# RWKV-7 and latent-attention mixers of a two-block model: deeper slots, smaller tiles, another order of the engines' work

## The reference

```python
def step(state, inp):                      # RWKV-7, 16 heads of 64, over 256 tokens
    r_t, w_t, k_t, v_t, a_t, b_t = inp
    sa = jnp.einsum('bhvk,bhk->bhv', state, a_t)
    state = (state * w_t[:, :, None, :]
             + sa[..., None] * b_t[:, :, None, :]
             + v_t[..., None] * k_t[:, :, None, :])
    return state, jnp.einsum('bhvk,bhk->bhv', state, r_t)

y = rwkv7_scan(r, decay, k, v, -kk, kk * a)        # then group norm, bonus, gate g
sc = (einsum(q_nope, k_nope) + einsum(q_pe, k_pe)) * scale     # MLA, 8 heads of 128
p = jax.nn.softmax(jnp.where(causal, sc, NEG_INF), axis=-1)
outs.append(jnp.einsum('bhqk,bkhd->bqhd', p.astype(v.dtype), v[:, :q1]))
x = x + jnp.concatenate([y_rwkv, y_mla], axis=-1) @ w_out[l]
```

## Time and profile before

| what | value |
|---|---|
| median of 3 runs | 2172.3 us |
| the profiled execution's own time | 2172.27 us |
| its span, first to last instruction | 2170.5 us |
| PE busy | 2147.1 us, 99% |
| DVE, ACT, POOL busy | 1689.5, 1089.1, 547.7 us |
| granted clock of PE | 0.999 of full |
| mixers stage | about 1223 to 1303 us |
| chain stage | about 1303 to 1325 us |

### The profile page before, as it was taken

How to read it: one execution, slowest core, us unless ns; L and a number is a source line. 1 busy time by engine, 2 the same in 40 slices (tenths; PEclk the granted TensorE clock), 3 DMA queues, 4 the chain that set the end, 5 groups by cost and what they waited for, 6 DMA issues and landing times.

```text
span 2170.5 us, 39431 instructions
## 1 busy us (share of the span) xinstructions
PE 2147.1 (99%) x14918; PEld 1881.1 (87%) x14918; DVE 1689.5 (78%) x2802; ACT 1089.1 (50%) x1489; POOL 547.7 (25%) x225
## 2 busy tenths in 40 slices
PE   8999999999999999999999999999999999999998
PEld 6888888888888888899999987888888888888887
DVE  7799778885899688788888656788888874547887
ACT  6555564445555564556554765443443443334454
POOL 4776731018677630210000623100000000000001
PEclk9999999999999999999999999999999999999999
DMA  7555445555545455554445302555555555555554
GB/s 260 189 177 182 163 175 177 191 192 196 189 170 184 152 184 184 185 205 159 159 165 188 118 25 97 193 178 190 191 180 190 192 181 189 193 181 187 193 213 175
DMA packets 69964, 384.82 MB, mean 177 GB/s; under 512 B 15376, under 2 KB 23056, under 8 KB 25168
## 3 DMA queue, kind: packets, MB, share of 16 engines
q1 hardware_dynamic: 69840, 383.09, 49.9%
HBM read 379.89 MB, written 3.18 MB: 176 GB/s over the span
## 4 chain that ended last, share of the span: by engine, by line
PE 71%; POOL 14%; issue 10%; DVE 2%; ACT 1%; DMA 1%; SPq 0%; POOLq 0%; DVEq 0%; ACTq 0%
PE ps L258 34%; PE ps L259 18%; POOL low L240 14%; PE ps L246 4%; PE ps L247 4%; PE ps L248 4%; PE ps L261 2%; DMA raw<-weights_dram 1%; PE ps L1898 0%; PE ps L1879 0%; PE ps L1865 0%; PE ps L1889 0%; PE ps L1939 0%; PE ps L2253 0%; PE ps L2255 0%
## 5 line engine op out<-in xcount | busy, mean ns | idle before, releaser
L258 PE MATMUL ps<-opA,whi 128*128 128x512 f32 x2460 | 871.2, 394 | 0.0
L259 PE MATMUL ps<-opA,low 128*128 128x256 f32 x2624 | 706.7, 279 | 0.2 <-DVE opA L1031 0.2
L228 ACT ACTIVATE whi<-raw 128x2048 fp32r<-128x2048 f32 x346 | 660.3, 1909 | 79.3 <-DMA raw<-weights_dram 78.0
L233 DVE TENSOR_TENSOR low<-raw,whi 128x2048 fp32r<-128x2048 f32 x252 | 583.4, 2315 | 65.0 <-ACT whi L228 51.2
L258 PEld LDWEIGHTS ps<-opA,whi 128*128 128x128 f32 x2460 | 461.1, 187 | 106.0 <-issue 3.0
L240 POOL TENSOR_TENSOR low<-raw,whi 128x2048 fp32r<-128x2048 f32 x94 | 432.0, 4613 | 408.0 <-ACT whi L228 378.7
L259 PEld LDWEIGHTS ps<-opA,low 128*128 128x128 f32 x2624 | 492.0, 187 | 14.6 <-DVE opA L1031 0.5
L258 PE MATMUL ps<-opB,whi 128*128 128x512 f32 x1380 | 493.3, 397 | 3.2 <-DVE small L1141 1.4
L259 PE MATMUL ps<-opB,low 128*128 128x256 f32 x1472 | 397.1, 280 | 0.0
L258 PEld LDWEIGHTS ps<-opB,whi 128*128 128x128 f32 x1380 | 259.4, 188 | 67.8 <-issue 5.0
L267 ACT ACTIVATE crossed<-ps 128x256 f32<-128x256 f32 x167 | 64.2, 384 | 488.7 <-PE ps L261 488.6
(11 more groups left out here) (431 smaller groups left out, 2583.1 us busy)
## 6 DMA issues: line engine op xcount, KB each, us to landing
raw<-weights_dram SPq DMA_DIRECT2D x348, 1024.0 KB, 4.8
bias_t<-table_dram SPq DMA_DIRECT2D x16, 384.0 KB, 5.9
raw<-weights_dram SPq DMA_DIRECT2D x4, 512.0 KB, 8.1
hT<-xT_dram SPq DMA_DIRECT2D x4, 512.0 KB, 8.3
lora_g<-lora_dram SPq DMA_DIRECT2D x1, 1024.0 KB, 5.0
out_dram<-y_tok SPq DMA_DIRECT2D x4, 256.0 KB, 2.4
out_dram<-hT SPq DMA_DIRECT2D x3, 256.0 KB, 2.7
p_in<-pT_dram SPq DMA_DIRECT2D x2, 256.0 KB, 5.8
```

The source lines that it names most:

```text
L228: act.activation(whi[:, v % RING, :], raw[:, v % RING, :], ACT.Copy).then_inc(hi_done.sem, 1)
L233: v_.tensor_tensor(wlo(v % RING, 0, width), raw[:, v % RING, 0:width], whi[:, v % RING, 0:width].bitcast(F32), ALU.subtract).then_inc(lo_d ...
L258: pe.matmul(*cross, start=start, stop=False)
L259: mm = pe.matmul(ps[:, b, 0:T], wlo(s, w0, w0 + P), op[:, k, 0:T], start=False, stop=False)
```

## The change

`keyed_values` of items 2 to 15 uses 32x32 tiles on the diagonal (the rest of the masked matrix is zero). `within_scores` takes its second and third operand, `kk` and `r_`, in one product of 64 columns; for that `kk` and `uS` become parts of one tile. The order inside the slots is another on PE, ACT and DVE: within-chunk scores are made two pairs ahead, `keyed_values` and `exps` one slot ahead, `turned` stands between the two keyed groups, `values` between the reads, and `steps(s)` ends slot s. The waits follow the new order. `gate_rows` is issued a slot later. An exponential of one element is put before the `k_pad` copy of the mix stage. The first state of the chain is copied once the first of the last four `step_out` is done, behind two `step_in`; the last `values` moves into the chain, behind the first next state, and the wait for the last store moves to the first `gates`.

```diff
@@ phase_mix, ACT
                 evict_block(6, 2)
+                act.activation(small[:, 3:4], small[:, 7:8], ACT.Exp)
                 act.wait_ge(*mx["k_rope"](1))
@@ phase_mixers, PE: within_scores, keyed_values, solved, reads, steps
-                        for x, (w, z) in enumerate(((a_gate, r_), (k_, kk), (k_, r_))):
+                        for x, w in enumerate((a_gate, k_)):
...
-                                    mm = pe.matmul(ps[CH * c:CH * c + CH, 3 + h, at:at + CH], w[head[h], pair, t], z[head[h], pair, t], start=True, stop=True)
+                                    z = kk_uS[head[h], pair:pair + apart + 1:apart, t] if x else r_[head[h], pair, t]
+                                    mm = pe.matmul(ps[CH * c:CH * c + CH, 3 + h, at:at + CH + CH * x], w[head[h], pair, t], z, start=True, stop=True)
...
-                        pe.wait_ge(*wi["ry_read"](n - 1))
+                        pe.wait_ge(*wi["aq_read"](n - 1))
...
+                        for c in range(4):
+                            t = slice(CH * c, CH * c + CH)
+                            mm = pe.matmul(ps[t, mine[y], cols], scm[t, pair % 2, y, h, 1, t], tokV[t, pair % 2, y, cols], start=True, stop=True)
...
+                    if n >= 2:
+                        pe.wait_ge(*wi["ry_read"](n - 1))
...
+                    if n + 2 < 2 * RW_B:
+                        pe.wait_ge(*wi["G_read"](n + 3))
...
+                    pe.wait_ge(*ml["probsT_read"](pair + 1))
                     if pair:
                         pe.wait_ge(*ml["stored"](pair))
...
+                    if pair + 1 < RW_B:
+                        pe.wait_ge(*ml["biased"](pair + 2))
@@ phase_mixers, ACT: order
+                keyed_read(0)
+                keyed_read(1)
+                exps(0)
+                scaled(0)
                 for s in range(RW_B):
                     more = s + 1 < RW_B
-                    keyed_read(2 * s)
-                    keyed_read(2 * s + 1)
-                    exps(s)
                     if s:
                         step_out(s - 1, 0)
                     solved_read(2 * s)
-                    solved_read(2 * s + 1)
                     if s:
                         step_out(s - 1, 1)
+                    solved_read(2 * s + 1)
                     if more:
                         tokens_read(2 * s + 2)
-                    scaled(s)
                     if s:
                         step_out(s - 1, 2)
                         step_out(s - 1, 3)
+                    if s in (3, 4):
+                        gate_rows(s - 3)
                     if more:
                         tokens_read(2 * s + 3)
+                        keyed_read(2 * s + 2)
+                        keyed_read(2 * s + 3)
+                        exps(s + 1)
...
-                    if s in (2, 3):
-                        gate_rows(s - 2)
+                    if more:
+                        scaled(s + 1)
@@ phase_mixers, DVE: order
                 biased(0)
+                masked(2)
+                masked(3)
+                finished(0)
...
-                    finished(s)
+                        if more:
+                            masked(2 * s + 3)
                     if more:
                         biased(s + 1)
-                        masked(2 * s + 2)
...
                     reads(2 * s)
+                    if s + 2 < RW_B:
+                        masked(2 * s + 4)
                     if more:
-                        masked(2 * s + 3)
+                        finished(s + 1)
                     reads(2 * s + 1)
...
-                for c in range(4):
-                    step_in(RW_B - 1, c)
+                step_in(RW_B - 1, 0)
+                step_in(RW_B - 1, 1)
+                v.wait_ge(*wi["held"](4 * (RW_B - 1) + 1))
+                v.wait_ge(*ml["outT"](MLA_H - 1))
+                v.tensor_copy(state[:, 1, :, :], step_n[:, 0, :, 0:DH]).then_inc(ch["state"].sem, 1)
+                step_in(RW_B - 1, 2)
+                step_in(RW_B - 1, 3)
@@ phase_chain, PE
+                        if c == 1 and todo == "next":
+                            last_values()
@@ phase_chain, DVE
                         v.wait_ge(*ch["next"](c))
+                        if c < 4:
+                            v.wait_ge(*wi["held"](4 * (RW_B - 1) + c + 1))
```

More of the change, by code:

```diff
@@ L1210, in program @@
         second = area + 2 * KB * T
-        uS = place("uS", [P, IN2_UNITS, T], at=arena)
+        apart = (arena - area) // T - 8
+        kk_uS = place("kk_uS", [P, apart + IN2_UNITS, T], at=area + 8 * T)
+        uS = kk_uS[:, apart:apart + IN2_UNITS, :]
         r_, k_, v_ = uS[:, 0:8, :], uS[:, 8:16, :], uS[:, 16:24, :]
@@ L1217, in program @@
         a_gate = place("a_gate", [P, RW_B, T], at=area)
-        kk = place("kk", [P, RW_B, T], at=area + 8 * T)
+        kk = kk_uS[:, 0:RW_B, :]
         bonus = place("bonus", [P, RW_B, T], at=area + 16 * T)
@@ L1790, in program @@
         step_n = uS[:, 8:24, :].rearrange("p (s n) t -> p s n t", s=2)
+        state = place("state", [P, 2, 2, RW_B, DH], at=second + 8 * T)[:, :, 0, :, :]
         def phase_mixers(u_next, op):
@@ L1976, in _ @@
                         scores(s + 1)
-                        within_scores(s + 1)
+                        tokens(2 * s + 3)
+                    if s + 2 < RW_B:
+                        within_scores(s + 2)
+                    if more:
+                        keyed_values(2 * s + 2)
+                    turned(s)
+                    if more:
+                        keyed_values(2 * s + 3)
                     reads(2 * s)
-                    if more:
-                        tokens(2 * s + 3)
-                    reads(2 * s + 1)
-                    turned(s)
                     if s:
                         values(s - 1)
-                steps(RW_B - 1)
+                    reads(2 * s + 1)
+                    steps(s)
                 pe.wait_ge(*ch["mla_lo"](1))
                 early_products(pe, u_next, 0, range(8, 12), op)
-                values(MLA_H - 1)
             @stage.scalar
@@ L2238, in gates, with last_values @@
                     mm.then_inc(ch["g"].sem, 1)
-                pe.wait_ge(*ml["stored"](MLA_H))
+                def last_values():
+                    pe.wait_ge(*ml["probsT_read"](MLA_H))
+                    pe.wait_ge(*ml["stored"](MLA_H - 1))
+                    pe.wait_ge(*wi["held"](4 * (RW_B - 1) + 3))
+                    pe.matmul(ps[:, 0, 0:T], vM[:, 0, 7 * P:8 * P], pTm[:, 1, 0:2, :], start=True, stop=False)
+                    mm = pe.matmul(ps[:, 0, P:T], vM[:, 1, 7 * P:8 * P], pTm[:, 1, 2, :], start=False, stop=True)
+                    mm.then_inc(ml["outT"].sem, 1)
                 for c in range(1, NCH):
@@ L2269, in _ @@
             def _(v):
-                v.wait_ge(*wi["held"](4 * RW_B))
-                v.wait_ge(*ml["outT"](MLA_H - 1))
-                v.tensor_copy(state[:, 1, :, :], step_n[:, 0, :, 0:DH]).then_inc(ch["state"].sem, 1)
                 v.wait_ge(*gs["w_hi"](2))
```

24 lines of the change are left out of this document (12 added, 12 removed).

## The result

The changed kernel takes 2178.2 us (median of 11 runs, 2175.6 to 2179.17), beside 2172.4 us for the kernel before on the same chip (11 runs, 2171.76 to 2173.94): a ratio of 1.0024, 95% interval 1.0016 to 1.0032. That is 5.8 us slower, where 0.8 faster was forecast, and outside the range. The profiled execution took 2178.3 us with a span of 2176.5.

A forecast was written before the change was run, and what follows sets the result against it. The prediction took TensorE (PE), busy for 99% of the span at full clock, to bound the kernel. Its terms, -4.4 + 0.2 + 2.7 - 1.2 + 1.9 = -0.8, gave 2171.5 us, range 2168.9 to 2174.3.

The forecast's parts named there:

- at nothing: Parts forecast to cost nothing: later gate rows, masked() further ahead, POOL's ends, one SP load, state's placement, kk joined to uS.
- 6, end of mixers: From solved(14) to the chain's first product: 7.9 us instead of 9.1, the last store's wait gone; -1.2 us.
- 1, keyed products: Keyed products of 14 items as 32x32 tiles: 0.22 us an item, 0.44 instead of 0.94 a slot, 0.50 saved.
- Rival A: Tiles don't run side by side: each keyed item costs 0.49 us, +3.8 over 14 items, 2175.3 us; 12%.
- 2, joined within-scores: Two within-score products joined, 32 products for 48: 0.72 us instead of 0.95 a slot, 0.23 saved.
- 3, order: Order in the slot: 0.21 us saved on step_out's wait, 0.20 lost to two more shape changes; period 9.05.
- 4, slot 6: Slot 6 has no within-scores left (-0.7), but steps(6) waits for store(5) behind ACT (+0.9); +0.2 us.
- 5, start: Start of the mixers: early exponential table load delays within-scores(0) by 1.1, tokens(3) waits about 0.9 for ACT; +2.7 us.
- 7, in the chain: Last values behind the chain's first product delay ACT's last store and first gate_w: 2.3 less 0.4 slack, +1.9 us.
- rival C: The chain's gate path has more slack than read, so its +1.9 falls away: -2.7, giving 2169.6 us; 10%.

The follow-up runs named there:

- lora_probs: The changed kernel with the gate's 1 MB load released by the turned probabilities of head 6, some 1.4 us later; 2174.16 us.
- pool_waits: lora_probs with POOL's subtraction into gw_stack held back until the chain's first state is copied; 2173.45 us.
- stack_early: lora_probs with ACT's gw_stack copy moved ahead of the store of the seventh head; 2174.19 us.
- gate_first: pool_waits with ACT doing the chain's first two gate_w pairs ahead of the two weight splits and the logarithm's table load; 2172.4 us.
- stack_gate: gate_first without the early exponential, and with ACT's gw_stack copy moved earlier in place of POOL's wait for the state; 2171.79 us.
- lora_outT: The changed kernel with the gate's 1 MB load released by the values of head 5, some 3.5 us later; 2174.24 us.
- before_gate_first: The kernel before, with ACT doing the first two gate_w pairs ahead of the two splits and the logarithm's table load; 2172.89 us beside 2172.62.
- values_first: lora_probs with the last values ahead of the chain's first next-state products instead of behind them; 2175.52 us.
- full_keyed: lora_probs with the keyed products of all 16 items full-size instead of in 32x32 tiles; 2179.27 us.
- gate_full: gate_first without the early exponential, all keyed products full-size, the gate's load behind the values of the sixth head; 2179.77 us.
- lora_halves: The changed kernel with the gate's 1 MB load in two of 0.5 MB, the second behind the values of the sixth head; 2175.1 us.
- before_lora_probs: The kernel before, with the gate's load released by the turned probabilities of head 6 instead of the scores of head 7; 2174.31 us.

## Why the prediction was wrong, step by step

**The loads, put at nothing, failed.** Under "at nothing" the prediction names one load, "SP's load behind the eighth mn, which leaves and lands about 1 us sooner"; that one did no harm. The load for the gate I did not look at: it too leaves at another point of PE's stream. I asked of the loads only when their data are wanted, and never what else uses the DMA engines. The price is 4.0 us, lora_probs against the change: 1.5 of PE's standstill, the rest the half clock behind it (from solved(14) to the state copy 10.11 us, 1295.87 to 1305.98, against 7.56 in lora_probs, 1294.34 to 1301.90). In the kernel before the packet came at 1288.3 and the load at 1289.8, so nothing in that trace spoke of it, but both were in it, 1.5 us apart.

With the load out of the way the time would have been 2174.2, inside the range, but not by the forecast's own sum: it lies 2.7 above it. The terms beside the load are compared in two stretches:

| stretch, us | before | forecast | change | lora_probs | pool_waits | stack_early | gate_first | stack_gate |
|---|---|---|---|---|---|---|---|---|
| solved(14) to the chain's first product | 9.12 | 7.9 | 11.96 | 9.41 | 8.05 | 9.03 | 8.04 | 9.04 |
| from there to the last kk | 20.31 | 22.2 | 22.47 | 22.45 | 22.45 | 22.45 | 21.95 | 21.30 |

**6, end of mixers (-1.2): the state copy mis-sized.** I took 0.5 us for the copy with its signal; it took 1.79. From the copy's start to the first product 1.85 us passed where I had 0.6. With the load out of the way the stretch is 0.3 longer than before (9.41) where I had it 1.2 shorter; with the copy at 0.43 it takes 8.05, close to the forecast's 7.9. I had moved a DVE operation by 1 us and not looked at what POOL does there. That the copy alone is not the price, but any DVE operation that meets POOL's, stack_early showed (9.03 with the copy at 0.43 and gw_lo at 2.21).

**1, keyed products (0.50 a slot): the size off.** An item costs 0.36 with the change of shape behind it, where I had 0.22 and 0.10, and the change ahead of turned 0.14 where I had 0.10. Of a gain of 0.30 (0.50 less two changes) 0.13 is left. Rival A was nearer, by another mechanism: the tiles cost less than its 0.49 an item, but the rest of the slot gives the gain back.

**2, joined within-scores (0.72):** right; 1242.02 to 1242.76 in lora_outT is 0.74. **3, order:** right in the best slots: a period of 9.09 (1276.11 to 1285.20 in the change) where I had 9.05. But the mean was 9.24, +0.95 over five periods. The first three took 9.34, 9.38 and 9.29; compared with slot 4 and 5, PE starts score products 0.2 to 0.3 us later in each of them, and one of these delays shows as a hole at issue (0.13 us at 1250.20). I had not expected such delays.

**4, slot 6 (+0.2):** steps(6) waited 0.44 us for ACT where I had 0.9, and its period is 8.96 in lora_probs where I had 9.25. **5, start (+2.7):** the waits came as forecast. Within-scores(0) wait 0.94 for the eviction, tokens(3) 1.14 for ACT:

```profile
1224.87 0.28 PE L1884 MATMUL ps<-kk_uS,a_gate 64*32 64x32 f32 x13 [0.94 <-ACT qT L1361]
...
1233.36 0.33 PE L1869 MATMUL ps<-ident,kk_uS 128*128 128x128 f32 x1 [1.14 <-ACT ends L2035]
```

+2.37 was measured to the first step_in, +2.7 forecast. No drain beyond the 1.28 us of the table load was seen, as I had read it: in the change it starts at 1222.63, 0.02 behind the eviction, and the exponential at 1223.92.

**7, in the chain (+1.9):** +2.16 measured, the first gate_w at 1316.37, 6.50 us behind the store, as forecast. The size was nearly right, but partly by luck, for the term has another composition. It puts all on the gate path, less a slack of 0.4 (its own two rows give 0.30). In the order before, the gate path costs nothing (before_gate_first), so rival C was right of that kernel; in the new one it costs 1.15 (22.45 in stack_early, 21.30 in stack_gate). The other 0.99 stays when nothing waits for gate_w (21.30 against 20.31 before). It fits the last values, 0.9 us of PE's own work, which now stand between the chain's first products: in values_first, with them ahead of the first product, the chain takes 20.53.

The terms as forecast would have made -0.8. The load adds 4.0 to 4.4, the copy 1.25, the slots 0.95, the rest nearly nothing: +5.6 in the profile, +5.8 in the medians.

## What to carry to other kernels

A change of order shifts transfers against PE's own instruction stream. Before such a change, list the large loads in the stretch and the instruction packets beside them; a packet that becomes due inside a load comes late, at worst at its end, and the price is the hole and perhaps a stretch at half clock. A well-chosen place of the load holds for one program only. Halves with a gap bound the delay to a half; one run speaks for them, 0.9 us slower than the well-chosen place.

An operation moved on DVE must be laid beside POOL's timeline, and the other way round: moving one only hands the collision to its neighbour, unless a true gap is found. And small tiles save time in their own group but cost records; a quarter less time per item was worth nothing here over six periods.

## What the runs showed of the hardware that I had not expected

- A packet of instructions that is due during a 1 MB load is late by up to the load's rest: packet and end of the load at 1293.0 and 1293.0 (the change), 1294.4 and 1294.4 (full_keyed), 1296.4 and 1296.5 (gate_full), 1291.9 at the end of the first half (lora_halves). PE then stood 1.5, 2.4 and 4.6 us, and not at all. In before_lora_probs and lora_outT the packet came inside the load, 2.1 and 1.3 us late, and the hole was 1.4 us and none.
- Lateness of 1.0 and 1.3 us gave no long hole, of 2.1 and 2.4 us holes of 1.4 and 1.5 us: PE had about 1 us of work in reserve. It went on 1.2 to 1.6 us after the packet had landed, in the long holes and in the small ones.
- The granted clock fell to half after the holes of 1.5, 2.4 and 4.6 us, and stayed there 6.8 us in the change. It stayed full after 1.4 us in before_lora_probs. What decides it in between was not tried.
- A DVE operation that meets a GpSimd operation, both on SBUF, waits for its end: 0.43 became 1.79, 1.22 became 2.21, 1.22 became 2.80. GpSimd's waits for DVE's in the same way: 2.36 became 3.27.
- Open: when the small holes come. They differ from program to program; that more records a slot bring more of them is argued from full_keyed and gate_full alone, which have one each (0.24 and 0.81 us). That the packets are PE's is read from their pace and from the holes, not from a name in the profile.
